# Differential attention's loop: the next weights' low part made by VectorE instead of GpSimd

## The reference

```python
sc = jnp.einsum('bqhcd,bkhcd->bhcqk', qblk, k)      # two score maps (c = 0, 1) for each of 8 heads
p = jax.nn.softmax(jnp.where(mask, sc, -jnp.inf), axis=-1)
a = p[:, :, 0] - lam * p[:, :, 1]
out = jnp.einsum('bhqk,bkhe->bqhe', a, vf)
...
o = rms_norm(o, subln_g) * (1.0 - lam_init)          # then @ w_out
```

## Time and profile before

| | before |
|---|---|
| time, median of 3 runs | 1287.05 us (1286.59 to 1292.16) |
| span of the profiled execution | 1291.9 us |
| PE, DVE, ACT, POOL busy, share of the span | 95%, 54%, 41%, 31% |
| heads 0 to 7 | about 677 to 884 us of the span |
| granted TensorE clock, mean of the span | 0.979 |

### The profile page before, as it was taken

How to read it: one execution, slowest core, us unless ns; L and a number is a source line. 1 busy time by engine, 2 the same in 40 slices (tenths; PEclk the granted TensorE clock), 3 DMA queues, 4 the chain that set the end, 5 groups by cost and what they waited for, 6 DMA issues and landing times.

```text
span 1291.9 us, 15912 instructions
## 1 busy us (share of the span) xinstructions
PE 1232.7 (95%) x5873; PEld 1007.7 (78%) x5873; DVE 700.7 (54%) x782; ACT 525.5 (41%) x663; POOL 403.5 (31%) x227
## 2 busy tenths in 40 slices
PE   6999999999999999999998887999999999999997
PEld 4888887878887888878986655667788878888876
DVE  5876666554443344456537777685544443354442
ACT  5554553343332233344225554665333332233343
POOL 4132123333330023334544343322233320043331
PEclk9999999999999999999998888999999999999999
DMA  5123223323323433223331210112233323333231
GB/s 151 49 66 97 81 67 109 91 75 97 97 74 97 122 98 97 73 80 107 98 99 33 65 33 32 33 65 66 71 107 93 87 86 106 101 98 97 61 101 66
DMA packets 192109, 107.66 MB, mean 83 GB/s; under 512 B 5981, under 2 KB 190534, under 8 KB 192070
## 3 DMA queue, kind: packets, MB, share of 16 engines
q1 hardware_dynamic: 189974, 107.09, 28.7%
q10 hardware_dynamic: 2096, 0.03, 0.1%
HBM read 105.01 MB, written 2.10 MB: 83 GB/s over the span
## 4 chain that ended last, share of the span: by engine, by line
PE 81%; DVE 8%; ACT 4%; issue 3%; POOL 3%; DMA 0%; SPq 0%; ACTq 0%; DVEq 0%; POOLq 0%
PE ps L1203 26%; PE ps L1204 25%; PE ps L1205 25%; DVE rsum L1127 1%; POOL mixF L466 1%; ACT w_hi L569 1%; DVE mixF L1130 1%; PE ps L1468 1%; ACT mixF L758 1%; DVE mixF L1132 1%; PE ps L1459 1%; DVE w_lo L846 1%; DVE rstd L863 1%; PE ps L1454 1%; DMA mixF<-in_x_dram 0%
## 5 line engine op out<-in xcount | busy, mean ns | idle before, releaser
L1203 PE MATMUL ps<-xs_hi,w_hi 128*128 128x512 f32 x960 | 387.6, 404 | 4.8 <-DVE mixF L1044 3.6
L1205 PE MATMUL ps<-xs_hi,w_lo 128*128 128x512 f32 x960 | 378.1, 394 | 0.0
L1204 PE MATMUL ps<-xs_lo,w_hi 128*128 128x512 f32 x960 | 378.0, 394 | 0.0
L569 ACT ACTIVATE w_hi<-wraw 128x2048 fp32r<-128x2048 f32 x112 | 213.7, 1908 | 190.2 <-PE ps L1205 181.2
L846 DVE TENSOR_TENSOR w_lo<-wraw,w_hi 128x2048 fp32r<-128x2048 f32 x104 | 239.2, 2300 | 64.8 <-ACT w_hi L569 62.9
L466 POOL TENSOR_TENSOR mixF<-mixF,rstd 128x512 f32<-128x512 f32 x44 | 120.0, 2727 | 380.8 <-ACT mixF L694 380.8
L1203 PEld LDWEIGHTS ps<-xs_hi,w_hi 128*128 128x128 f32 x960 | 183.0, 191 | 46.8 <-DVE mixF L1044 4.4
L1204 PEld LDWEIGHTS ps<-xs_lo,w_hi 128*128 128x128 f32 x960 | 182.8, 190 | 38.9 <-issue 2.9
L1205 PEld LDWEIGHTS ps<-xs_hi,w_lo 128*128 128x128 f32 x960 | 182.5, 190 | 39.0
L1203 PE MATMUL ps<-h_hi,w_hi 128*128 128x512 f32 x480 | 189.2, 394 | 7.3 <-POOL h_lo L469 5.9
L1205 PE MATMUL ps<-h_hi,w_lo 128*128 128x512 f32 x480 | 186.9, 389 | 0.0
(11 more groups left out here) (194 smaller groups left out, 1474.3 us busy)
## 6 DMA issues: line engine op xcount, KB each, us to landing
wraw<-in_ffn_w_up_dram SPq DMA_DIRECT2D x88, 512.0 KB, 4.9
wraw<-in_ffn_w_down_dram SPq DMA_DIRECT2D x32, 384.0 KB, 3.9
wraw<-in_ffn_w_down_dram SPq DMA_DIRECT2D x32, 320.0 KB, 3.7
wraw<-in_mlstm_w_in_dram SPq DMA_DIRECT2D x16, 512.0 KB, 4.9
wraw<-in_w_kv_dram SPq DMA_DIRECT2D x16, 512.0 KB, 5.0
wraw<-in_mlstm_w_in_dram SPq DMA_DIRECT2D x16, 256.0 KB, 3.0
wraw<-in_mlstm_w_out_dram SPq DMA_DIRECT2D x8, 512.0 KB, 4.0
wraw<-in_diff_w_q_dram SPq DMA_DIRECT2D x8, 512.0 KB, 3.9
```

The source lines that it names most:

```text
L569: act.activation(w_hi[:, s, :], wraw[:, s, :], ACT.Copy).then_inc(w_hi_made, 1)
L1203: pe.matmul(o, w[0], m[0], start=start, stop=False)
L1204: pe.matmul(o, w[0], m[1], start=False, stop=False)
L1205: return pe.matmul(o, w[1], m[0], start=False, stop=stop)
```

## The change

POOL's `weights_lo` and its call at the head of POOL's `attn` go. DVE's `attn` gets a call of its own `weights_lo` as its first instruction, ahead of the first maximum. It is the same subtraction of the same 128 x 2048 elements, with the same wait for `w_hi` and the same semaphore. As the slot has to be a constant, DVE's loop over heads 1 to 6 now has two heads in its body.

```diff
-            def weights_lo(u, s):
-                pool.wait_ge(w_hi_made, u + 1)
-                pool.tensor_tensor(w_lo[:, s, :], wraw[:, s, :], f32(w_hi[:, s, :]), ALU.subtract)\
-                    .then_inc(w_split, 1)
-
             def attn(h, s, scale=True, nxt=True, prev=True):
 
-                weights_lo(h + (U_QK + 2), 1 - s)
                 if prev:
                     attn_o_lo(h - 1)
...
-            def attn(h, prev=True, nxt=True):
+            def attn(h, s, prev=True, nxt=True):
+                weights_lo(h + (U_QK + 2), s)
                 attn_max(h, 0)
                 attn_max(h, 1)
...
-            attn(0, prev=False)
-            with dve.Fori(1, HB - 1) as h:
-                attn(h)
-            attn(HB - 1, nxt=False)
+            attn(0, 0, prev=False)
+            with by_two(dve, 1, HB - 1) as h:
+                attn(h, 1)
+                attn(h + 1, 0)
+            attn(HB - 1, 1, nxt=False)
```

## The result

The changed kernel takes 1303.39 us (median of 9 runs, 1301.03 to 1304.94), the kernel before, run beside it, 1286.73 us (median of 9, 1284.38 to 1296.91). The ratio is 1.0105 with a 95% interval of 1.0078 to 1.0132: slower by some 13.5 us. The forecast was slower by 7.5 us. The ratio times the 1287.05 us of the forecast is 1300.6 us, inside the range; the median itself lies 2.4 us above it. The profiled execution of the changed kernel had a span of 1299.4 us and a time of 1301.12 us, so what lies around the span is 1.7 us.

A forecast was written before the change was run, and what follows sets the result against it. PE's matmuls were taken to bound the whole span, with PE waiting for the softmax in the attention. Heads 1 to 7 at +11.5 us and head 0 at -4.0 gave +7.5 on 1287.05: 1294.6 us, range 1287.5 to 1301.

The forecast's parts named there:

- The stall of L1127: DVE's 128x2 multiplication in each head, held by POOL's subtraction: 2.32 us to fall to 0.16 us.
- the logarithm in its stead: ACT's late logarithm releases transpose 0: 1.71 us later in heads 1 to 4, 1.57 in 5 to 7, together +11.5 us.
- The new PE gap: PE idle about 1.5 us ahead of scores 2 and 0.5 us ahead of transpose 0.
- Head 0: First head, without a previous one: expected to gain 4.0 us, between 1.7 and 4.6.
- Scaling, stall and delay: Head 0: POOL scales from 674.5, holds DVE's L1111 to 678.4, and scores 0 come 1.5 us late.
- I expect the clock to stay up: Head 0: PE's 3.68 us idle ahead of transpose 0 shrinks to about 0.5, keeping full clock; another 1.95 us gained.
- a second low stretch: Rival: new PE idle at scores 2 lowers the clock again in heads 1 to 7, 1298 to 1310 us; chance 0.11.
- The prediction's last sign of being wrong: The prediction is wrong if the clock's low stretches change in number.
- The clock giving time back: Rival: low clock stretches in heads 1 to 4 vanish or shrink, 1284 to 1292 us; chance 0.22.
- the mix or PE sets transpose 0: Rival: transpose 0 waits for PE's path (1290.8 us) or the mix (1285.2 us), not the logarithm; chance 0.06.
- The hidden subtraction: Rival: DVE's subtraction is hidden and only the stall's end remains, about 1278 us; chance 0.05.

The follow-up runs named there:

- e1: Changed kernel with ACT's logarithm of the previous head moved ahead of the exponentials of row block 1; 1308.64 us, 1.0160 of before.
- e2: Changed kernel with DVE's subtraction moved from ahead of the first maximum to behind the low part of transpose 3; 1286.59 us, 0.9975 of before.
- e10: Changed kernel with the subtraction behind the four maxima of row blocks 0 and 1, ahead of mix 0; 1288.33 us, 0.9979 of before.
- e6: Kernel before with the change in head 0 alone, POOL still subtracting in heads 1 to 7; 1289.62 us, 0.9985 of before.
- e9: Changed kernel without POOL's scaling of units 3 to 7 in the attention's loop; 1283.38 us, 0.9957 of before.
- e8: Kernel before without POOL's scaling of units 3 to 7 in the attention's loop; 1268.56 us, 0.9833 of before.
- e7: Changed kernel with head 0's subtraction left with POOL, heads 1 to 7 as changed; 1306.26 us, 1.0109 of before.
- e11: Changed kernel with the subtraction behind transpose 3's low part and POOL's scaling ahead of the previous head's, held until mix 1 is done; 1268.17 us, 0.9805.
- e4: Changed kernel with POOL's scaling moved ahead of the previous head's low part; 1292.87 us, 1.0027 of before.

## Why the forecast came out as it did

**The direction and the mechanism were right.** The stall of L1127 went, and DVE's place ahead of the maxima put the logarithm in its stead: forecast 1.71 and 1.57 us per head, measured 1.84 in heads 1 to 4 and 1.5 us in heads 5 to 7, +11.9 us in place of +11.5. That the logarithm releases transpose 0 stands in the profile after, and e1 shows it: with the logarithm earlier the distance shrinks by 0.8 and 0.7 us. e2 and e10 show that the place is the cost. The forecast time was right only by its range: 7.5 us were forecast and some 13.5 measured, and the 1300.6 us by the ratio lie 0.4 us below its upper end.

**The new PE gap.** Forecast 1.5 us ahead of scores 2 and 0.5 us ahead of transpose 0, measured 1.38 and 0.69 us.

**Head 0 was mis-sized.** The term was -4.0 us and measured -2.0 us in the profiles (e6 by time: not told from nothing). Scaling, stall and delay came as worked out. The step that failed is "I expect the clock to stay up". I looked only at the gap of 3.68 us that goes. That scores 0 are 1.5 us late makes another for PE ahead of them, 0.81 us grown to 2.26, and behind it the clock fell. Scores 0 to transpose 0 then took 9.14 us, and transpose 0 came 0.5 us later than before in place of 1.7 us earlier. From transpose 0 to 2 head 0 won 2.9 us (6.16 in place of 9.04), more than the 1.95 us that I had.

**The term that was missing is the clock.** I set the sum on the median and the half clock as equal on both sides, while my own bounds had +2.6 to +18 us for "a second low stretch" with a chance of 0.11. That rival came true in part, on top of the forecast. The prediction's last sign of being wrong, low stretches that change in number, came true with it: seven in heads 0 to 7 in place of five. In the profiled execution the half clock now reaches the front of heads 2 and 4, and transposes 0 to 1 take 3.55 us there in place of 2.93:

```profile
736.00:741.00 5.00, 5.00 (x26) 3.27 (x24) 3.47 (x9) 3.58 (x8) 0.00 (x0) 0.66 0.58 155
```

In these two heads that costs 1.2 us. In heads 1 and 3 a shorter stretch behind transpose 3 gave 2.1 us back, so that in this execution the clock does not cost heads 1 to 4 anything over before. Over the runs the balance is against the change: 42 of 69 runs of before keep a mean clock of 0.983 or more, none of the changed kernel does, and that is about 5 of the 13.5 us. e9 against e8 shows falls that come with the new wait and without the gap at transpose 3. Its price could have been bounded before: the profiled span stood 4.9 us above the median, and I read that as the clock; what I didn't ask is whether the changed kernel could still have runs with as few falls. By e6 and e7 the lack of such runs belongs to heads 1 to 7. That the new wait is its cause is argued and not shown: the runs other than the profiled one have no trace, and two kernels without this wait ahead of scores 2 seldom reach 0.983 either (e2 in 5 of 12 runs, none above 0.984; e10 in 2 of 12). An edit also moves the heads against each other in time, and what that does to the clock is left open.

**The rivals.** The clock giving time back (0.22) is seen in heads 1 and 3 of the profiled execution only. That the mix or PE sets transpose 0 (0.06) is out by the profile. The hidden subtraction (0.05) would have needed another place: e2 is that kernel, and it is faster by 0.25% only.

## What to carry to other kernels

A subtraction that stalls a neighbour through a shared port was not made cheaper here by giving it to the neighbour at the head of its queue: what counts is which instructions are queued behind it, and DVE had room for it elsewhere. Before such a move, list for the receiving engine its idle time and what released the end of it; idle time ahead of the moment when the input is ready hides nothing. Where an engine stalls beside another, place the second one's work over instructions that don't need the shared port (here those that read PSUM): with the subtraction late that was worth some 18 us (e2's 1286.59 us against e11's 1268.17), while the change itself lost 13.5. And where a kernel's runs spread with the clock, compare the clocks of the runs, not the profile of one of them.

## What was not expected of the hardware

How long PE is idle before does not by itself say whether TensorE's granted clock falls to the half, 1.2 GHz. Gaps of 2.15 to 2.28 us ahead of head 0's scores went before a fall in eight profiles of eight. But the 3.27 us at transpose 3 did so in heads 1 to 4 of the kernel before and not in heads 1 to 3 of e7, where the clock had fallen and risen again before that gap (a mean of 0.52 from 712 to 715 us and 1.00 from 727 to 735). And gaps of about 1.3 and 0.5 us ahead of scores 2 and transpose 0 leave heads 5 to 7 of the changed kernel at the full clock (1.00 from 817 to 884 us), while head 6 of e9 and heads 5 to 7 of e4, with the same 1.3 us ahead of scores 2, have falls (0.50 from 829 to 831 us; 0.94 from 803.5 to 857 us). Gaps of 1.0 us alone brought none (e8: 1.00 over seven heads). Runs of the same program are up to 13 us apart, and most of that goes with their mean clock (0.975 to 0.991).
